# A ninth weight buffer in the room of the attention's buffers, the last w_down chunks in halves, and a split combine

## The chip, the cores and the metric

The kernel runs on one core of a Trainium2 chip. The metric is the time of one launch on the device in microseconds (us). The core has a matrix engine (TensorE, PE in the rows; its weight loads are PEld), a vector engine (VectorE, DVE), an activation engine (ScalarE, ACT), GpSimd (POOL) and SyncE (SP), which here issues every transfer (DMA) from the device's memory (HBM). The engines run their own lists of instructions and wait for each other by semaphores. SBUF is the memory on the core, with 128 partitions; matmul results go to PSUM, eight banks of 128 x 512 floats.

## What is computed

A trunk of two layers on 256 tokens of width 1024. Each layer is an attention (layer 0: a mix of three branches; layer 1: plain causal attention over one block, as there is only one) and then a mixture of experts, each followed by a layer norm of a residual sum. The change concerns the experts:

```
def grouped_moe(h, router_w, router_bias, w_gate, w_up, w_down):
    ...
    for e in range(N_EXPERTS):          # 16 experts, 2 chosen for each token
        he = jax.nn.silu(xt @ w_gate[e]) * (xt @ w_up[e])
        out = out + (he @ w_down[e]) * gate[:, e:e + 1]

def reference(x, ...):
    for layer in range(DEPTH):          # 2
        mix = nsa_mixer(...) if layer == 0 else moba_mixer(...)
        x = layer_norm(DN_ALPHA * x + mix, ...)
        ffn = grouped_moe(x, router_w, router_bias, w_gate[layer], w_up[layer], w_down[layer])
        x = layer_norm(DN_ALPHA * x + ffn, ...)
```

All is float32. `w_gate` and `w_up` are 1024 x 512 for each expert, `w_down` is 512 x 1024: 2 MiB each, 96 MiB for a layer's experts, all of which are read.

## The kernel before

**The ring.** Weights pass through `ring`, eight slots of 2 MiB (a chunk: 16 KB in each of 128 partitions). `STREAM` lists all chunks in the order of their loading: nine of layer 0's attention, 48 of its experts (`("moe", 0)` to `("moe", 47)`), eight of layer 1's attention (`("unit", 7)` to `("unit", 14)`), 48 of its experts. Chunk number c of the stream goes to slot c % 8, and SyncE issues its load when the chunk eight places before it has been used (`slot_free`, `wait_consumed`). An expert chunk is one DMA (L336), an attention chunk two of 1 MB (L313). Each slot has two semaphores for landings, one for each half; an expert chunk uses the first alone.

**The experts' rounds.** A stage has eight rounds (`PAIRS`), each of two experts, whose tokens (up to 64 each) are computed side by side in two halves of the array. A round takes six chunks, k = 0 to 5: w_gate of both experts, w_up of both, w_down of both. So chunk 6 i + k belongs to round i. On the TensorE a round (`experts`) is

- 32 matmuls with w_gate (`to_hidden`, L612), transposes of the gates of its slots (L618);
- 32 matmuls with w_up (L612);
- `combine` of the round before (L640): 8 matmuls that add its results to the tokens in PSUM banks 4 to 7, four for each half w of the columns;
- transposes of the hidden rows (L623), after the DVE has multiplied them (L1238); the DVE then copies them (L1241);
- in rounds 0 to 5 gathers of tokens for later rounds (L602);
- 32 matmuls with w_down (`from_hidden`, L630), for which ACT (L841) and the DVE (L1249) then make a scaled high part and the rest, one instruction for each half w;
- in rounds 0 to 5 more gathers.

The w_down block goes through the row blocks k and in each through both column halves w; in the last round it does all of w = 0 first, so that ACT and DVE can begin with that half in the middle of the block. After round 7 comes a last `combine`, then the layer norm.

**Before the stage.** Attention uses two further buffers, `R5` and `R6` (3072 floats in each partition): probabilities, transposed probabilities, staging for the rotary part, and last `OT`, its result, in the upper part of both. The output matmuls (`mix_out`, L562) read `OT` and count up `L.mix`, to 4 in a layer. The layer norms keep their weights in the first 2048 floats of `R5`; the experts keep `GP`, gate values by slot, in the first 512 of `R6`. SyncE issues expert chunks 0 to 5 early, and 6 and 7 behind the attention's last probabilities; both wait for `mix_out`, since their slots hold its weights. Then it waits for the layer norm (`x_ready`), loads the weights of the next one, and goes on with chunk 8, which waits for round 0's gate matmuls (`gate_done`).

## Time and profile before

| | us |
|---|---|
| median of 3 runs | 820.42 |
| lowest, highest | 819.17, 820.86 |
| the profiled execution | 817.06 |
| its span | 815.3 |
| TensorE busy in it | 754.2 |

The profile is of one execution. Its span is the time between the first and the last instruction of the core; 1.8 us lie outside it. All moments below are counted from the span's start. Layer 0's expert stage runs on the TensorE from 205.9 to 423.5 us, layer 1's from 586 to 804.7. A block of 32 matmuls stands in the rows as one row with its start, its duration and, in brackets, how long the engine was idle before it and what ended that.

### The profile page before, as it was taken

How to read it: one execution, taken by the hardware profiler on the slowest of the kernel's cores; microseconds unless marked ns; L12 is line 12 of the kernel's file. 1: busy time of each engine (PE TensorE's matmuls, PEld its weight loads, DVE VectorE, ACT ScalarE, POOL GpSimd, SP SyncE). 2: the span in 40 equal slices, each digit the busy share in tenths (PEclk: the TensorE clock that was granted, in tenths of full speed). 3: DMA queues.
4: the chain of work that ended last, by engine and by line, in shares of the span. 5: the costliest groups of instructions: out<-in, count | busy, mean ns of one | idle time of the engine just before them, and what ended most of it. 6: DMA issues, size and time to landing. Idle time of an engine off the chain costs nothing.

```text
span 815.3 us, 9027 instructions
## 1 busy us (share of the span) xinstructions
PE 754.2 (93%) x3713; PEld 402.3 (49%) x3713; DVE 282.5 (35%) x564; ACT 187.8 (23%) x435; POOL 88.0 (11%) x96
## 2 busy tenths in 40 slices
PE   5999999998999999998878999899899999998884
PEld 4877855545434444343236887555634344443331
DVE  3594365326212211111146874523521122111114
ACT  3443456312111001100004445612200110011000
POOL 0011234312000000000000320411200000000000
PEclk9999789999999999999997999999899999999997
DMA  9999400106599999999999854013489999999981
GB/s 297 366 391 411 188 1 2 52 15 243 201 430 427 428 429 426 428 427 427 429 388 386 328 207 174 34 52 110 148 353 427 428 428 425 430 427 428 428 347 53
DMA packets 38924, 245.03 MB, mean 301 GB/s; under 512 B 5344, under 2 KB 9568, under 8 KB 26592
## 3 DMA queue, kind: packets, MB, share of 16 engines
q1 hardware_dynamic: 38880, 244.41, 74.2%
q8 instruction: 32, 0.52, 0.3%
q14 instruction: 12, 0.10, 0.0%
HBM read 243.35 MB, written 1.05 MB: 300 GB/s over the span
## 4 chain that ended last, share of the span: by engine, by line
PE 79%; DMA 8%; DVE 7%; ACT 3%; issue 2%; POOL 0%; DVEq 0%; SPq 0%
PE ps L612 24%; PE ps L630 12%; DMA ring<-in_w_up 8%; PE ps L562 7%; PE ps L435 5%; PE ps L436 4%; PE ps L437 4%; PE ps L602 3%; PE ps L640 3%; PE ps L484 2%; ACT R L943 2%; PE ps L472 2%; PE ps L593 1%; PE ps L569 1%; PE ps L418 1%
## 5 line engine op out<-in xcount | busy, mean ns | idle before, releaser
L612 PE MATMUL ps<-ring,R 128*64 128x512 f32 x1024 | 229.9, 602 | 17.4 <-DMA ring<-in_w_up 7.9
L612 PEld LDWEIGHTS ps<-ring,R 128*64 128x64 f32 x1024 | 75.4, 138 | 150.6 <-issue 149.0
L630 PE MATMUL ps<-ring,R 128*64 128x512 f32 x512 | 113.4, 595 | 3.1 <-DVE R L1241 3.1
L841 ACT ACTIVATE wh<-ps,small 128x512 fp32r<-128x512 f32 x32 | 22.0, 687 | 276.1 <-PE ps L630 274.5
L1078 DVE TENSOR_TENSOR wl<-ring,wh 128x512 fp32r<-128x512 f32 x88 | 66.5, 770 | 48.3 <-ACT wh L819 48.1
L435 PE MATMUL ps<-wh,xh 128*128 128x512 f32 x176 | 71.9, 409 | 5.0 <-DVE wl L1078 4.9
L436 PE MATMUL ps<-wl,xh 128*128 128x512 f32 x176 | 70.4, 400 | 0.0
L437 PE MATMUL ps<-wh,xl 128*128 128x512 f32 x176 | 70.4, 400 | 0.0
L630 PEld LDWEIGHTS ps<-ring,R 128*64 128x64 f32 x512 | 35.3, 137 | 69.6 <-issue 64.0
L819 ACT CAST wh<-ring 128x512 fp32r<-128x512 f32 x88 | 54.3, 621 | 58.3 <-PE ps L437 58.3
L1249 DVE SCALAR_TENSOR_TENSOR wl<-ps,small,wh 128x512 fp32r<-128x512 f32 x32 | 24.0, 751 | 104.3 <-ACT wh L841 103.6
L562 PE MATMUL ps<-ring,R 128*128 128x512 f32 x128 | 56.8, 597 | 0.0
L1238 DVE TENSOR_TENSOR R<-R,ps 128x512 f32<-128x512 f32 x16 | 17.2, 1075 | 114.3 <-PE ps L612 114.3
L1245 DVE TENSOR_SCALAR wl<-ps 128x256 fp32r<-128x256 f32 x16 | 6.8, 424 | 115.4 <-PE ps L618 115.4
L943 ACT ACTIVATE R<-ps,small 128x128 f32<-128x128 f32 (+1 forms) x96 | 39.0, 419 | 29.7 <-DVE small L1128 29.7
L435 PEld LDWEIGHTS ps<-wh,xh 128*128 128x128 f32 x176 | 33.8, 192 | 15.0 <-DVE xl L1073 4.9
L986 POOL TENSOR_TENSOR R<-wh,small 128x512 f32<-128x512 f32 x8 | 8.3, 1043 | 284.6 <-PE ps L618 272.0
L437 PEld LDWEIGHTS ps<-wh,xl 128*128 128x128 f32 x176 | 33.6, 191 | 8.2
L436 PEld LDWEIGHTS ps<-wl,xh 128*128 128x128 f32 x176 | 33.8, 192 | 7.7
L562 PEld LDWEIGHTS ps<-ring,R 128*128 128x128 f32 x128 | 23.7, 190 | 27.6 <-issue 26.8
L1128 DVE TENSOR_REDUCE small<-ps 128x2 f32<-128x256 f32 (+1 forms) x48 | 24.5, 553 | 35.7 <-PE ps L472 35.7
L1011 POOL TENSOR_TENSOR R<-R 128x512 f32<-128x512 f32 (+1 forms) x16 | 23.3, 1459 | 123.9 <-DVE R L1121 123.9
(152 smaller groups left out, 812.9 us busy)
## 6 DMA issues: line engine op xcount, KB each, us to landing
ring<-in_w_gate SPq DMA_DIRECT2D x32, 2048.0 KB, 18.7
ring<-in_w_up SPq DMA_DIRECT2D x32, 2048.0 KB, 20.1
ring<-in_w_down SPq DMA_DIRECT2D x32, 2048.0 KB, 22.5
ring<-in_w_in SPq DMA_DIRECT2D x22, 1024.0 KB, 14.0
ring<-in_w_out SPq DMA_DIRECT2D x8, 1024.0 KB, 14.9
ring<-in_cmp_kw SPq DMA_DIRECT2D x2, 1024.0 KB, 16.3
ring<-in_cmp_vw SPq DMA_DIRECT2D x2, 1024.0 KB, 13.3
R<-in_ln_g SPq DMA_DIRECT2D x4, 512.0 KB, 5.1
```

Of the source, the lines that this page charges most:

```text
L435: mm(to, xh[:, j, tok], wh[:, c % WBUF], start=(j == 0), stop=False)
L436: mm(to, xh[:, j, tok], wl[:, c % WBUF], start=False, stop=False)
L437: last = mm(to, xl[:, j, tok], wh[:, c % WBUF], start=False, stop=(j == KJ - 1))
L562: last = mm(ps[:, 2 * a + w, :], OT[j][:, a * P:(a + 1) * P], in_slot(("unit", u))[:, j * UNIT:(j + 1) * UNIT], start=False, stop=(j == KJ ...
L602: last = mm(ps[:, bank, at * n:(at + 1) * n], Xp[k][:, a, j, :], Pm[:, a].rearrange("p e c -> p (e c)")[:, 0:n], start=(a == 0 and k == 0) ...
L612: last = mm(ps[64 * e:64 * e + 64, to, :], xe[:, j, at + 64 * e:at + 64 * e + 64], slots[e][:, j * UNIT:(j + 1) * UNIT], start=(j == 0), s ...
L630: last = mm(ps[64 * e:64 * e + 64, 2 + w, :], hT[:, k, 64 * e:64 * e + 64], slots[e][:, at:at + UNIT], start=(k == 0), stop=(k == FJ - 1))
L640: last = mm(ps[:, 4 + 2 * a + w, :], PmT[:, b, a, :], Yp[k][w], start=False, stop=(k == 1), skip_group_check=True)
L819: copy(wh[:, c % WBUF], in_slot(("unit", u))[:, j * UNIT:(j + 1) * UNIT]).then_inc(w_hi, 1)
L943: last = nc.scalar.activation(to, ps[:, 2 * (m % 2) + a, c:c + w], ACT.Exp, bias=nmax[:, m % 2, t, a:a + 1], accum_out=sums[:, m % 3, t, a ...
L1078: tt(wl[:, c % WBUF], in_slot(("unit", u))[:, j * UNIT:(j + 1) * UNIT], wh[:, c % WBUF], ALU.subtract).then_inc(w_lo, 1)
L1128: last = nc.vector.tensor_reduce(nmax[:, m % 2, t, :], ps[:, b:b + 2, t * P:t * P + (t + 1) * P], AX.X, ALU.max, negate=True)
```

## The change

- `R5` and `R6` become the two parts of one buffer `R56` of 6144 floats. Its last 4096 floats (the last third of `R5` and all of `R6`) are a ninth slot, `extra`. `GP` moves to the last quarter of `R4`.
- `places_of_stream` gives each chunk its slot. Chunk 8 of each expert stage goes to the ninth slot, which nothing of the stream held before; it waits until `L.mix` has reached 4. From then on each chunk takes the slot of the chunk nine before it. When attention chunks come, the ninth slot leaves the rotation.
- SyncE issues chunk 8 right behind chunk 7, ahead of its wait for the layer norm.
- The last two chunks of a stage, w_down of both experts of round 7, are loaded in halves of 1 MB (rows of the block k = 0, 1 first, for both experts, then k = 2, 3). The w_down block of round 7 goes through the halves one after the other, in each through w = 0 and w = 1, and waits for the second halves in its middle.
- In rounds 6 and 7 `combine` is split: its half w = 0 stays where it was, its half w = 1 comes behind the transposes of the hidden rows.

```diff
+        R56 = sb("R56", [P, 6 * D])
+        R5, R6 = R56[:, 0:3 * D], R56[:, 3 * D:6 * D]
+        extra = R56[:, 2 * D:6 * D]
...
-        GP = R6[:, 0:512].rearrange("p (a e c) -> p a e c", a=T, e=4)
+        GP = R4[:, 3 * FE:4 * FE].rearrange("p (a e c) -> p a e c", a=T, e=4)
...
+        LASTDOWN = 6 * PAIRS - 2
+
+        def places_of_stream():
+            slots, before, line = [], [], [(None, n) for n in range(SLOT)]
+            for what in STREAM:
+                if what[0] == "moe" and what[1] % (6 * PAIRS) == SLOT:
+                    held, n = None, SLOT
+                else:
+                    if what[0] != "moe":
+                        line = [x for x in line if x[1] != SLOT]
+                    held, n = line.pop(0)
+                slots.append(n)
+                before.append(held)
+                line.append((what, n))
+            return slots, before
+
+        SLOT_OF, BEFORE = places_of_stream()
+        in_halves = lambda what: what[0] != "moe" or what[1] % (6 * PAIRS) >= LASTDOWN
...
             def slot_free(what):
-                if AT[what] >= SLOT:
-                    wait_consumed(sp, STREAM[AT[what] - SLOT])
+                if BEFORE[AT[what]]:
+                    wait_consumed(sp, BEFORE[AT[what]])
+                elif SLOT_OF[AT[what]] == SLOT:
+                    l = what[1] // (6 * PAIRS)
+                    sp.wait_ge(L.mix, base[l].mix + 2 * T)
...
+                if in_halves(what):
+                    if k == 5:
+                        for h in range(2):
+                            for e in range(2):
+                                to = ("moe", n - 1 + e)
+                                c = slice(2 * D * h, 2 * D * (h + 1))
+                                sp.dma_start(in_slot(to)[:, c], expert_src(l, 2 * i + e, 2)[:, c]).then_inc(landing(to, h)[0], 16)
+                    return
                 sp.dma_start(in_slot(what), expert_src(l, 2 * i + k % 2, k // 2)).then_inc(landing(what, 0)[0], 16)
...
-                for n in range(ahead, 8):
+                for n in range(ahead, SLOT + 1):
                     load_expert(6 * PAIRS * l + n)
                 sp.wait_ge(N.x_ready, ready(2 * l, T - 1, 1))
                 load_ln(2 * l + 1, R.ln_in)
-                for n in range(8, 6 * PAIRS):
+                for n in range(SLOT + 1, 6 * PAIRS):
                     load_expert(6 * PAIRS * l + n)
...
                     if i:
-                        combine(rd, (i - 1) % 2, (2 * n - 1, 2 * n))
+                        combine(rd, (i - 1) % 2, (2 * n - 1, 2 * n), range(2) if more else (0,))
                     pe.wait_ge(rd.h, n + 1)
                     transpose_hidden(rd)
                     if more:
                         pe.wait_ge(rd.onehot, g + 2)
                         gather(rd, 1, (2 * part, 2 * part + 1), 4 * SLOTS)
+                    else:
+                        combine(rd, (i - 1) % 2, (2 * n - 1, 2 * n), (1,))
...
-                    from_hidden(rd, slots[4:6], [(k, w) for k in range(FJ) for w in range(2)] if i < PAIRS - 1 else
-                                [(k, w) for w in range(2) for k in range(FJ)])
+                    if i < PAIRS - 1:
+                        from_hidden(rd, slots[4:6], [(k, w) for k in range(FJ) for w in range(2)])
+                    else:
+                        from_hidden(rd, slots[4:6], [(k, w) for h in range(2) for w in range(2) for k in (2 * h, 2 * h + 1)],
+                                    chunks[4:6])
```

SyncE's list before, from the attention's end of layer 0 into the first rounds. The words in brackets name the semaphores waited for: `pt` counts the attention's transposed probabilities, `mix` its output matmuls, `ln_x_ready` the layer norm, the last three the gate, up and w_down blocks:

```order
L340 DMA R<-in_ln_g 128x1024 [waits pt]
L341 DMA R<-in_ln_b 128x1024
L336 DMA ring<-in_w_gate 128x4096 [waits mix] x2
L340 DMA R<-in_ln_g 128x1024 [waits ln_x_ready]
L341 DMA R<-in_ln_b 128x1024
L336 DMA ring<-in_w_up 128x4096 [waits gate_done_main] x2
L336 DMA ring<-in_w_down 128x4096 [waits up_done_main] x2
L336 DMA ring<-in_w_gate 128x4096 [waits y_main] x2
```

And after (the ninth slot shows as `R`):

```order
L372 DMA R<-in_ln_g 128x1024 [waits pt]
L373 DMA R<-in_ln_b 128x1024
L368 DMA ring<-in_w_gate 128x4096 [waits mix] x2
L368 DMA R<-in_w_up 128x4096 [waits mix]
L372 DMA R<-in_ln_g 128x1024 [waits ln_x_ready]
L373 DMA R<-in_ln_b 128x1024
L368 DMA ring<-in_w_up 128x4096 [waits gate_done_main]
L368 DMA ring<-in_w_down 128x4096 [waits gate_done_main]
L368 DMA ring<-in_w_down 128x4096 [waits up_done_main]
L368 DMA ring<-in_w_gate 128x4096 [waits up_done_main]
```

One w_up chunk stands ahead of the layer norm's wait now, and the pairs that wait for one block are shifted by one chunk.

The TensorE in round 7 of layer 0 before, from the end of the w_up block (L612) to the last combine (L640):

```order
L612 MATMUL ps<-ring,R 64x512 x15
L640 MATMUL ps<-wh,wl 128x512 [waits y_lo_main]
L640 MATMUL ps<-wl 128x512
L640 MATMUL ps<-wh,wl 128x512
L640 MATMUL ps<-wl 128x512
L640 MATMUL ps<-wh,wl 128x512 [waits y_lo_main]
L640 MATMUL ps<-wl 128x512
L640 MATMUL ps<-wh,wl 128x512
L640 MATMUL ps<-wl 128x512
L623 MATMUL ps<-cst,R 128x128 [waits h_main]
L623 MATMUL ps<-cst,R 128x128 x3
L630 MATMUL ps<-ring,R 64x512 [waits landed7_0,landed0_0,gsum_main,ht_sb_main]
```

And after, from the same block's end (L675 is `combine`, L655 the transposes, L665 the w_down block):

```order
L675 MATMUL ps<-wh,wl 128x512 [waits y_lo_main]
L675 MATMUL ps<-wl 128x512
L675 MATMUL ps<-wh,wl 128x512
L675 MATMUL ps<-wl 128x512
L655 MATMUL ps<-cst,R 128x128 [waits h_main]
L655 MATMUL ps<-cst,R 128x128 x3
L675 MATMUL ps<-wh,wl 128x512 [waits y_lo_main]
L675 MATMUL ps<-wl 128x512
L675 MATMUL ps<-wh,wl 128x512
L675 MATMUL ps<-wl 128x512
L665 MATMUL ps<-ring,R 64x512 [waits landed2_0,landed3_0,gsum_main,ht_sb_main]
L665 MATMUL ps<-ring,R 64x512 x7
```

Four of the eight combine matmuls moved behind the transposes. The lists of ACT and the DVE are the same as before but for the names of slots.

## Rows read from the trace of the kernel before

**Rows 1.** The page: header, TensorE's busy time, and GB/s in 40 slices.
```profile
span 815.3 us, 9027 instructions
...
PE 754.2 (93%) x3713; PEld 402.3 (49%) x3713; DVE 282.5 (35%) x564; ACT 187.8 (23%) x435; POOL 88.0 (11%) x96
...
GB/s 297 366 391 411 188 1 2 52 15 243 201 430 427 428 429 426 428 427 427 429 388 386 328 207 174 34 52 110 148 353 427 428 428 425 430 427 428 428 347 53
```

**Rows 2.** Chain of waits, 335 to 436 us: start, duration, what.
```profile
371.41 31.98 DMA ring<-in_w_up
```

**Rows 3.** Timeline of PE, layer 0's last rounds: start, duration, matmuls [idle before].
```profile
344.34 7.09 PE L612 MATMUL ps<-ring,R 128*64 128x512 f32 x32 [1.64 <-issue]
...
373.75 7.09 PE L612 MATMUL ps<-ring,R 128*64 128x512 f32 x32 [2.38 <-DMA ring<-in_w_up]
...
393.73 8.68 PE L612 MATMUL ps<-ring,R 128*64 128x512 f32 x32 [2.53 <-DMA ring<-in_w_gate]
...
403.53 7.09 PE L612 MATMUL ps<-ring,R 128*64 128x512 f32 x32 [0.75 <-DMA ring<-in_w_up]
...
413.90 7.09 PE L630 MATMUL ps<-ring,R 128*64 128x512 f32 x32 [0.78 <-DVE R L1241]
```

**Rows 4.** Timeline of PE, round 7 of layer 1.
```profile
773.19 7.09 PE L612 MATMUL ps<-ring,R 128*64 128x512 f32 x32 [2.11 <-DMA ring<-in_w_gate]
...
782.99 8.61 PE L612 MATMUL ps<-ring,R 128*64 128x512 f32 x32 [2.34 <-DMA ring<-in_w_up]
...
794.86 7.09 PE L630 MATMUL ps<-ring,R 128*64 128x512 f32 x32 [0.79 <-DVE R L1241]
```

**Rows 5.** Timeline of SyncE's queue: issues of chunks 6, 7 and 8, 9.
```profile
181.32 9.86 SPq L336 DMA_DIRECT2D ring<-in_w_gate  x2
...
213.06 0.80 SPq L336 DMA_DIRECT2D ring<-in_w_up  x2
```

**Rows 6.** Busy time by stretch; last three columns: clock, DMA share, GB/s.
```profile
210.00:214.00 4.00, 4.00 (x22) 1.26 (x18) 0.58 (x2) 0.60 (x1) 0.00 (x0) 1.00 0.00 0
232.00:342.00 110.00, 110.00 (x534) 44.77 (x530) 20.04 (x30) 10.25 (x17) 2.09 (x2) 1.00 1.01 428
```

**Rows 7.** Issues of ring in four stretches, each with its time to landing.
```profile
L336 SPq DMA_DIRECT2D ring<-in_w_gate x1: 328/328/328, 190.8 to 190.8; - x1
...
DMA to landing us min/median/max: 8.0/8.0/8.0
...
L336 SPq DMA_DIRECT2D ring<-in_w_up x2: 327/376/425, 371.0 to 371.4; - x2
...
DMA to landing us min/median/max: 27.5/29.7/32.0
...
L336 SPq DMA_DIRECT2D ring<-in_w_down x2: 328/380/432, 380.9 to 381.2; - x2
...
DMA to landing us min/median/max: 27.4/29.7/32.0
...
L313 SPq DMA_DIRECT2D ring<-in_w_in x2: 382/552/721, 391.2 to 391.7; - x2
...
DMA to landing us min/median/max: 24.7/25.8/27.0
```

**Rows 8.** Busy time by stretch at layer 1's last w_up block; columns as rows 6.
```profile
783.00:787.00 4.00, 4.00 (x12) 1.38 (x14) 0.00 (x0) 0.00 (x0) 0.00 (x0) 0.61 0.99 422
```

**Rows 9.** Timeline of all engines in round 7 of layer 0.
```profile
410.73 1.10 DVE L1238 TENSOR_TENSOR R<-R,ps 128x512 f32<-128x512 f32 x1 [7.16 <-PE ps L612]
...
412.52 0.60 PE L623 MATMUL ps<-cst,R 128*128 128x128 f32 x4
...
413.16 0.69 DVE L1241 COPY R<-ps 128x512 f32<-128x512 f32 x1 [1.33 <-PE ps L623]
...
421.04 0.69 ACT L841 ACTIVATE wh<-ps,small 128x512 fp32r<-128x512 f32 x1 [2.69 <-PE ps L630]
...
421.76 0.75 DVE L1249 SCALAR_TENSOR_TENSOR wl<-ps,small,wh 128x512 fp32r<-128x512 f32 x1 [2.62 <-ACT wh L841]
```

More of the change, by code:

```diff
@@ L111, in build @@
         R4 = sb("R4", [P, T * D])
-        R5 = sb("R5", [P, 3 * D])
-        R6 = sb("R6", [P, 3 * D])
+        R56 = sb("R56", [P, 6 * D])
+        R5, R6 = R56[:, 0:3 * D], R56[:, 3 * D:6 * D]
+        extra = R56[:, 2 * D:6 * D]
         small = sb("small", [P, 832])
@@ L194, in build @@
         x_in, ident_in, c_in, s_in = sem("x_in"), sem("ident_in"), sem("c_in"), sem("s_in")
-        landed = [[sem(f"landed{s}_{h}") for h in range(2)] for s in range(SLOT)]
+        landed = [[sem(f"landed{s}_{h}") for h in range(2)] for s in range(SLOT + 1)]
         w_hi, w_lo, w_used = sem("w_hi"), sem("w_lo"), sem("w_used")
@@ L238, in build @@
         AT = {what: c for c, what in enumerate(STREAM)}
+        LASTDOWN = 6 * PAIRS - 2
[14 more added lines that the diff above has]
+        in_halves = lambda what: what[0] != "moe" or what[1] % (6 * PAIRS) >= LASTDOWN
         def in_slot(what):
-            return ring[:, AT[what] % SLOT]
+            n = SLOT_OF[AT[what]]
+            return ring[:, n] if n < SLOT else extra
         def landing(what, h):
             c = AT[what]
-            n = sum(1 for b in range(c % SLOT, c + 1, SLOT) if h == 0 or STREAM[b][0] != "moe")
-            return landed[c % SLOT][h], 16 * n
+            n = sum(1 for b in range(c + 1) if SLOT_OF[b] == SLOT_OF[c] and (h == 0 or in_halves(STREAM[b])))
+            return landed[SLOT_OF[c]][h], 16 * n
         def wait_consumed(eng, what):
@@ L624, in transpose_hidden, with from_hidden @@
                 last.then_inc(rd.ht, 1)
-            def from_hidden(rd, slots, order):
-                for k, w in order:
+            def from_hidden(rd, slots, order, second=None):
+                for n, (k, w) in enumerate(order):
+                    if second and n == 4:
+                        for to in second:
+                            pe.wait_ge(*landing(to, 1))
                     for e in range(2):
@@ L633, in from_hidden, with combine @@
                         last.then_inc((rd.y0, rd.y)[w], 1)
-            def combine(rd, b, counts):
-                for w in range(2):
+            def combine(rd, b, counts, ws=range(2)):
+                for w in ws:
                     pe.wait_ge(rd.y_lo, counts[w])
```

## The prediction

> **What bounds the kernel now.** I read the page first: its header and the line of GB/s in 40 slices [rows 1]. The TensorE is busy 93% of 815.3 us, so one would look for matmuls to save; but the GB/s line says that in two long stretches (slices 12 to 20 and 31 to 38, in the two expert stages) the transfers run flat at about 428 GB/s. Two resources are near full there, and which of them ends the stage has to be read from its end. For that I took the chain of waits over the end of layer 0's experts [rows 2]: one link, 31.98 us from the issue of the last w_up chunk to 403.4 us, is a transfer. The timeline of the TensorE shows the same from its side [rows 3]: from round 5 of 8 on it stands idle before blocks of 32 expert matmuls, 1.64, 2.38, 2.53 and 0.75 us, and the releaser of the last three is a chunk of weights (for the first the row shows none; nothing else is missing there but a chunk). Layer 1 repeats it 380 us later [rows 4]. So each expert stage begins bound by the TensorE (which starts with eight chunks in the ring) and ends bound by the transfers. The other engines are no candidates: they wait for the TensorE throughout.
>
> What sets the end of the transfers? The SyncE's list [rows 5]: chunks 6 and 7 of the stage are issued at 181.32 and 9.5 us later (the row's 9.86 us span both, the second's issue being the last 0.33), then nothing until 213.06, when round 0's gate block has freed the first slots. In that gap the transfers stand still: 0 GB/s in 210 to 214 us [rows 6]. From 213 us on they never pause (428 GB/s over 232 to 342 us). Landing times, worked out as issue plus time to landing [rows 7]: the last two w_up chunks at 371.03 + 27.5 = 398.5 and 371.41 + 32.0 = 403.4, the last two w_down chunks at 380.87 + 27.4 = 408.3 and 381.24 + 32.0 = 413.2 us. The step is **4.9 us per chunk**, and it holds for the whole stage: a lone chunk takes 8.0 us from issue to landing [rows 7], 3.1 more than a step, so chunk 8 landed at 213.06 + 8.0 = 221.1, and the 39 steps to 413.2 average 4.93. So the last landing is 213 us plus the latency plus as many steps as chunks are still to come.
>
> **The change part by part.** *Ninth buffer.* Chunk 8 of each stage no longer waits for the gate block of round 0 but for the attention's last output matmul, as chunk 7 does, and is issued right behind it. It lands one step behind chunk 7 (190.8 + 8.0 = 198.8), at 204 us, in a gap that lasts to 213 [rows 5, 6]: its transfer is hidden. On the SyncE it stands ahead of two small loads (layer-norm weights, which the DVE needs at the end of the stage, 200 us later) and adds no wait that chunk 7 hasn't. From 213 us on 39 chunks are left, not 40; the slot for each comes from the chunk nine before, and the stream is never short of a free slot: the order of freeing is the same, one chunk later in number. So each landing from there on comes **4.9 us** earlier. Is the TensorE early enough to use it? Its waits on chunks up to the last w_up block add up to 1.64 + 2.38 + 2.53 + 0.75 = 7.3 us [rows 3]; 4.9 of these may go before it becomes the bound, and 2.4 are left. In layer 1 the waits before the last gate and up blocks are 2.11 and 2.34 [rows 4], 4.5 us by themselves, and earlier ones come on top. So the last up block starts at 403.53 - 4.9 = 398.6 in layer 0. Value 4.9 per layer; 0 is the floor if nothing lands earlier, and more than 4.9 is excluded as one chunk is moved.
>
> *Split of combine in rounds 6 and 7.* After the up block (over at 403.53 + 7.09 = 410.6) the TensorE runs 8 combine matmuls, done at 412.5, then the transposes of the hidden rows from 412.52; but the DVE had the hidden rows ready at 410.73 + 1.10 = 411.83 [rows 9]. With 4 of the 8 ahead (1.0 us) the TensorE is free at 411.6, waits for the DVE and transposes from 411.87: 0.65 us sooner. The DVE copies the transposes 0.64 us behind their start and takes 0.69 [rows 9], to 413.20; the TensorE runs the other 4 combine matmuls meanwhile, from about 412.35 to 413.35. So the last w_down block starts at 413.35 where it was 413.90: **0.55 us** gained. From below 0 bounds it, if the second half of the combine costs all of it; from above 0.65. I take 0.55, as every piece has its row. In round 6 the split gains nothing: the next gate block waits for its chunk (2.53 us [rows 3]).
>
> *Halves of the last two w_down chunks.* Without them the w_down block could start when both have landed, 413.2 - 4.9 = 408.3; the TensorE gets there at 398.6 + (413.35 - 403.53) = 408.4. The two nearly coincide, so the halves save nothing if all goes as worked out, and make sure that the split's 0.55 is kept: the first halves land by 403.4, the second by 408.3, and the second are needed only after half the block, 3.5 us later. Their cost: four issues where two were, some 0.4 us each on a queue with nothing urgent behind it, and perhaps slower packets. The nearest rows are the 1 MB loads of w_in, the first two of which land at 391.2 + 24.7 = 415.9 and 391.7 + 27.0 = 418.7 [rows 7], 2.7 to 2.8 us apart where half a chunk's step is 2.45. Four at 2.8 take 11.2 for 9.8: 1.4 us, inside the 3.5 of cover. Value 0; what would make it a loss is rival D.
>
> The Trainium skill has a rule against this part: by "SBUF — State Buffer", section "The DMA setup-cost knee", each transfer pays a fixed 2 us or so beside its bytes, and one large transfer is to be preferred. By it two more transfers would bring the last landing to 412.3, 0.4 us behind the 411.9 at which it is needed. The sum would then be 0.8 us less gain in both layers together. The rows speak against it: chunks that stand in the queue land 4.9 us apart where a lone one takes 8.0 [rows 7], so the fixed part is paid once.
>
> *Order of the last block.* Column half 0 is now finished after three quarters of the block, not after one half, 1.75 us before its end. ACT and DVE need 0.69 and 0.75 us for it [rows 9] and some 0.1 of signals, so it is ready 0.2 us before the block's end. No cost; were it missed, 0.2.
>
> *Moved buffer GP and the next layer's loads.* GP goes to another free place with the same instruction; 0. The loads of layer 1's first weights (issued from 391.2 on [rows 7]) now wait for a chunk one earlier and come behind the last w_down: they land 4.9 us sooner, as all does. 0.
>
> **Sum.** 2 x (4.9 + 0.55) = 10.9 us. The profiled execution took 817.06 (span 815.3), so it would take 806.2. The runs shown have their median at 820.42, 3.4 us over the profiled one; nothing in the sum depends on where these 3.4 lie, so I subtract from the median: **809.5 us**.
>
> **What may disturb it: the clock.** The granted clock falls to its lower level (1.2 for 2.4 GHz) behind some of the waits: in layer 0 the gate block behind the 2.53 us wait took 8.68 us and not 7.09 [rows 3]; in layer 1 it was the last up block, 8.61 us behind 2.34 us [rows 4], with the clock at 0.61 over 783 to 787 us [rows 8]. Waits of 2.38 and 2.11 us had no such effect. The first fall was absorbed by the next wait for a chunk; the second was paid in full, 1.52 us, since behind the last up block nothing waits for a transfer any more. After the change the wait before that block is 9.8 - 7.09 - 0.44 = 2.3 us as before, in both layers. So anything from no fall paid (808.0) to both (811.0) can come; one, as now, is the middle.
>
> **Rivals.**
> A, only the buffer pays: the second part of the combine or a late w_down eats the 0.55. 820.42 - 9.8 = 810.6. For it: the two times that nearly coincide (408.3 and 408.4). Against: halves.
> B, one fall of the clock more is paid on the last blocks or in the routing between attention and experts, and the split gives nothing: 810.6 + 1.5 = 812.1.
> C, each half costs 1.0 us beside its bytes, a third of the 3.1 that a lone chunk shows over its step: the last one lands at 408.3 + 4.0 = 412.3, 0.4 us late in each layer, 809.5 + 0.8 = 810.3. For it: the w_in loads' 0.3 each, which is too little; against it: the queued chunks. This is also where the skill's rule above would end.
> D, slower: the halves do not overlap, and each of the four pays the 3.1 us that a lone chunk shows over its step [rows 7]. They then take 4 x (2.45 + 3.1) = 22.2 us behind the last w_up chunk, and the last lands at 398.5 + 22.2 = 420.7, where it is needed at 411.9: 8.8 us late per layer, against a gain of 5.45. That gives 820.42 + 2 x 3.35 = 827.1. It decides from 411.9 + 5.45 = 417.4 on, that is if each half costs some 2.3 us beside its bytes. Against it speak all queued chunks, 4.9 us apart.
> E, the change does not do what it says: the ninth chunk is not away before 213 us, because SyncE stands elsewhere. Only the split is left: 820.42 - 1.1 = 819.3. Against: the SyncE was free at about 191.5 us.
>
> **How the numbers follow.** Chances: forecast 0.65 (808.0 to 811.0 with the clock's share), A 0.15, B 0.12, C 0.03, D 0.02, E 0.03. The range takes in the forecast with a fall less and its rounding (1.5 more below for what the median's distance from the profile leaves open) and A, B and C above: 806.5 to 813.0. It leaves out D, E and a little of each tail. Faster by over 0.2% (1.6 us, about what a measurement of this kernel can tell from no change) are the forecast, A, B and C: 0.95; same is E: 0.03; slower is D: 0.02.
>
> **What would show it.** In the profile after: a ninth chunk issued beside chunk 7 and no pause shorter than before 213; last w_up chunk landing near 398.5 in layer 0, last up block starting there; 4 combine matmuls, transposes, 4 combine matmuls, and 9.8 us from the last up block's start to the w_down block's where it was 10.4; layer 1 shifted by 5.4 at its start and the last w_down block by 10.9. I am wrong if the TensorE no longer waits for chunks in rounds 6 and 7 (then it is the bound, and less than 4.9 was to be had), if the stream after 213 us has pauses, or if the waits are the same and blocks longer.

## The result

The changed kernel takes 809.05 us (median of 4 runs, 805.87 to 809.25), the kernel before, on the same chip, 820.64 (819.17 to 820.92). The ratio is 0.9861, 95% interval 0.9841 to 0.9881: 11.4 us less by the ratio and 11.6 between the medians, where 10.9 were forecast, and the time is 0.5 us from the 809.5 predicted.

The page of after shows the same kernel with the same flat stretches in the transfers:

```profile
span 807.4 us, 9035 instructions
...
PE 757.7 (94%) x3713; PEld 404.5 (50%) x3713; DVE 282.3 (35%) x564; ACT 187.8 (23%) x435; POOL 88.0 (11%) x96
...
GB/s 301 365 394 379 231 2 1 1 52 242 190 431 428 428 427 426 428 426 427 425 397 387 400 160 157 105 53 98 267 251 429 427 427 427 429 427 427 427 388 54
```

SyncE's queue, timeline of after, which answers to [rows 5]:

```profile
184.13 9.86 SPq L368 DMA_DIRECT2D ring<-in_w_gate  x2
194.03 0.43 SPq L368 DMA_DIRECT2D R<-in_w_up  x1
197.46 0.33 SPq L372 DMA_DIRECT2D R<-in_ln_g  x1
197.83 0.45 SPq L373 DMA_DIRECT2D R<-in_ln_b  x1
217.22 0.33 SPq L368 DMA_DIRECT2D ring<-in_w_up  x1
217.59 7.34 SPq L368 DMA_DIRECT2D ring<-in_w_down  x2
```

The third issue, `R<-in_w_up`, is chunk 8, at 194.03, and the view of this one issue has its time to landing:

```profile
L368 SPq DMA_DIRECT2D R<-in_w_up x1: 432/432/432, 194.0 to 194.0; - x1
...
DMA to landing us min/median/max: 12.6/12.6/12.6
```

At 206.6 it is there, 10.6 us before the next issue. The two small loads are issued 3.4 us behind it, still in the pause. That is the forecast picture.

The end of layer 0's stage, timeline of PE in after, answers to [rows 3] and [rows 9] (L644 is `to_hidden`, L655 the transposes, L675 `combine`, L665 `from_hidden`):

```profile
393.36 8.64 PE L644 MATMUL ps<-ring,R 128*64 128x512 f32 x32 [2.70 <-DMA ring<-in_w_gate]
...
403.16 0.62 PE L644 MATMUL ps<-R 128*64 128x512 f32 x1 [0.80 <-DMA ring<-in_w_up]
...
411.50 0.66 PE L655 MATMUL ps<-cst,R 128*128 128x128 f32 x4
411.91 0.48 PE L675 MATMUL ps<-wh,wl 128*128 128x512 f32 x1
...
413.01 7.09 PE L665 MATMUL ps<-ring,R 128*64 128x512 f32 x32
```

Here the TensorE still waits for chunks in round 7, so the stage is bound by the transfers as before, one step earlier. From the last w_up block (403.16) to the last w_down block (413.01) it is 9.85 us where it was 10.37. The last w_up chunk lands 192.9 us behind the start of layer 0's stage where it was 197.5, and 191.9 behind that of layer 1's where it was 196.8: 4.5 and 4.9 us earlier. Layer 1's last gate block fell to the lower clock in this run, and not its last up block:

```profile
767.34 8.78 PE L644 MATMUL ps<-ring,R 128*64 128x512 f32 x32 [2.62 <-DMA ring<-in_w_gate]
```

**Where the profiled span moved.** Both profiles can be cut at the first gate block of each stage and the last w_down block (the stretch between them is called the stretch below). A stage starts with the row of its first gate block, here in after's timeline, where it was 205.93 before:

```profile
210.09 7.09 PE L644 MATMUL ps<-ring,R 128*64 128x512 f32 x32
```

| piece of the span | before | after | difference |
|---|---|---|---|
| start to layer 0's stage | 205.93 | 210.09 | +4.16 |
| stretch, layer 0 | 207.97 | 202.92 | -5.05 |
| to layer 1's stage | 172.11 | 172.08 | -0.03 |
| stretch, layer 1 | 208.85 | 201.87 | -6.98 |
| rest | 20.4 | 20.4 | 0.0 |

The sum is -7.9 and not -10.9, because the part ahead of the first stage, of whose instructions none was changed, took 4.2 us more. Its cause stands in the clock column (last but two) of the busy time by stretch. Before:

```profile
80.00:115.00 35.00, 33.94 (x248) 0.76 0.31 131
195.00:206.00 11.00, 9.40 (x64) 0.84 0.52 194
```

and after:

```profile
80.00:115.00 35.00, 34.00 (x232) 0.71 0.34 145
195.00:210.00 15.00, 12.14 (x68) 0.77 0.84 334
```

The TensorE was granted less clock there in this execution. Matched matmul by matmul, after falls behind before in three places only: by 1.4 us between 15 and 17 us (matmuls 0.45 us apart in before are 0.85 apart in after), by 1.5 between 84 and 87, and by 1.5 between 195 and 203. How much of these stretches runs at the lower clock differs from one execution to the next. It was so in all the profiles below too: layer 0's stage began between 203.97 and 210.25 us in kernels whose instructions up to there are the same but for SyncE's issue of chunk 8. That issue isn't the cause either: without the early chunk the stage began at 203.97 to 210.25 us (four profiles), with it at 204.90 to 210.17 (ten). The median over several runs averages this, one profile doesn't: the two stretches are the better measure of the change. In layer 1, 1.52 of the 6.98 are the fall that [rows 4] showed on before's last up block, gone from there in this run, so the change itself made 5.05 and 5.46 us.

### The profile page after: what moved, and what is told of

Same layout as the page of the kernel before. It is cut to its first block, busy times and chain, and to the rows that moved or that the text cites. A ratio compares the mean times of both kernels' runs of the same rounds, so it can differ in the third digit from the quotient of the medians.

```text
span 807.4 us, 9035 instructions
## 1 busy us (share of the span) xinstructions
PE 757.7 (94%) x3713; PEld 404.5 (50%) x3713; DVE 282.3 (35%) x564; ACT 187.8 (23%) x435; POOL 88.0 (11%) x96
## 4 chain that ended last, share of the span: by engine, by line
PE 80%; DMA 8%; DVE 7%; ACT 3%; issue 2%; DVEq 0%; SPq 0%
PE ps L644 24%; PE ps L665 12%; DMA ring<-in_w_up 7%; PE ps L594 7%; PE ps L467 5%; PE ps L468 5%; PE ps L469 4%; PE ps L634 3%; PE ps L675 3%; ACT R L983 2%; PE ps L504 2%; PE ps L516 2%; PE ps L625 1%; PE ps L607 1%; PE ps L450 1%
## 5 line engine op out<-in xcount | busy, mean ns | idle before, releaser
L644 PE MATMUL ps<-ring,R 128*64 128x512 f32 x928 | 230.0, 603 | 5.3 <-DMA ring<-in_w_gate 5.3
L644 PEld LDWEIGHTS ps<-ring,R 128*64 128x64 f32 x928 | 72.2, 139 | 115.9 <-issue 114.0
L665 PE MATMUL ps<-ring,R 128*64 128x512 f32 x448 | 113.4, 596 | 0.8 <-DMA ring<-in_w_down 0.8
L665 PEld LDWEIGHTS ps<-ring,R 128*64 128x64 f32 x448 | 35.4, 137 | 67.4 <-issue 63.5
L644 PE MATMUL ps<-R 128*64 128x512 f32 x96 | 42.4, 595 | 1.4 <-DMA ring<-in_w_up 1.4
```

Of the source, the lines that this page charges most:

```text
L644: last = mm(ps[64 * e:64 * e + 64, to, :], xe[:, j, at + 64 * e:at + 64 * e + 64], slots[e][:, j * UNIT:(j + 1) * UNIT], start=(j == 0), s ...
L665: last = mm(ps[64 * e:64 * e + 64, 2 + w, :], hT[:, k, 64 * e:64 * e + 64], slots[e][:, at:at + UNIT], start=(k == 0), stop=(k == FJ - 1))
```

## The experiments

The runs were made in five groups, each on one chip together with the kernel before; "before" is its median in that group, and times of different groups are compared by their ratios. The time is the measure for the whole. The stretch is the measure for parts of a microsecond; it comes from one profiled execution of each kernel, and where the same kernel was profiled twice (after), the two differ by 0.26 and 0.08 us.

| kernel | time us | before | ratio (95%) | stretch 0 | stretch 1 |
|---|---|---|---|---|---|
| before | - | - | - | 207.97 | 208.85 (fall) |
| after | 809.05 | 820.64 | 0.9861 (0.9841 to 0.9881) | 202.92 | 201.87 |
| after once more | 807.57 | 820.49 | 0.9836 (0.9810 to 0.9862) | 202.66 | 201.95 |
| ninth buffer only | 808.32 | 820.01 | 0.9857 (0.9827 to 0.9887) | 203.29 | 202.79 |
| split only | 817.53 | 820.01 | 0.9968 (0.9947 to 0.9989) | 207.67 | 206.88 |
| without halves | 808.94 | 820.01 | 0.9866 (0.9835 to 0.9897) | 202.75 | 202.02 |
| ninth late | 824.18 | 820.01 | 1.0066 (1.0040 to 1.0091) | 212.78 (fall) | 210.35 |
| ninth late, clean | 818.52 | 820.49 | 0.9974 (0.9956 to 0.9993) | 207.62 | 206.98 |
| chunks 9, 10 in halves | 806.85 | 820.49 | 0.9837 (0.9811 to 0.9864) | 202.28 | 201.41 |
| chunks 9, 10 in quarters | 805.43 | 820.49 | 0.9812 (0.9786 to 0.9837) | 201.85 | 201.64 |
| chunks 9 to 14 in halves | 804.98 | 821.16 | 0.9800 (0.9766 to 0.9833) | 201.97 (fall) | 200.75 (fall) |
| chunks 9 to 20 in halves | 806.72 | 821.16 | 0.9824 (0.9793 to 0.9855) | 201.23 (fall) | 201.50 (fall) |
| w_up of round 7 in halves | 808.25 | 821.21 | 0.9851 (0.9831 to 0.9870) | 201.89 | 199.57 |
| 9 to 14 and w_up in halves | 796.57 | 821.21 | 0.9720 (0.9696 to 0.9744) | 197.96 | 196.62 |

"Fall" marks a stretch whose last up block ran in part at the lower clock.

### One part alone

**The ninth buffer alone.** The changed kernel with two things put back:

```diff
-        in_halves = lambda what: what[0] != "moe" or what[1] % (6 * PAIRS) >= LASTDOWN
+        in_halves = lambda what: what[0] != "moe"
...
-                        combine(rd, (i - 1) % 2, (2 * n - 1, 2 * n), range(2) if more else (0,))
+                        combine(rd, (i - 1) % 2, (2 * n - 1, 2 * n))
...
-                    else:
-                        combine(rd, (i - 1) % 2, (2 * n - 1, 2 * n), (1,))
...
-                        from_hidden(rd, slots[4:6], [(k, w) for h in range(2) for w in range(2) for k in (2 * h, 2 * h + 1)],
-                                    chunks[4:6])
+                        from_hidden(rd, slots[4:6], [(k, w) for w in range(2) for k in range(FJ)])
```

> The ninth buffer with its early chunk alone; w_down chunks whole, combine unsplit. The measure that the clock disturbs least is the stretch from the start of round 0's gate block to the start of round 7's w_down block, 207.97 us in layer 0 of before and 208.78 in layer 1 (1.52 of them a fall of the clock on the last up block). Theory (the early chunk shifts the whole stream by one step, the split adds 0.55 per layer): stretch about 203.1 to 203.4 in layer 0, time 9.8 us under before, about 810.8. Rival (the split carries a good part of the gain): less than 8 us under before.

Measured: 203.29 in layer 0, 4.68 us under before, 202.79 in layer 1, 4.54 under before without its fall, and 808.32 us, ratio 0.9857. The buffer with its early chunk carries nearly the whole change.

**The split alone**, in the kernel before: `combine` takes the halves as an argument, and rounds 6 and 7 call it with (0,) ahead of the transposes and (1,) behind them.

> The kernel before with combine split in rounds 6 and 7 and nothing else. Theory: the last w_down block starts 9.8 us behind the start of the last up block where it is 10.37, if its chunk is there. Without the ninth buffer the last w_down chunk lands 9.8 us behind the last w_up chunk, so the gain is 0.4 to 0.55 us per layer, 0.8 to 1.1 in the time: about 819.7, hardly more than the spread of the runs. Rival: 0, because the chunk is late; then the row of the w_down block names a transfer as its releaser.

Measured: stretches of 207.67 and 206.88, that is 0.30 and 0.45 us gained (with 1.52 for the fall taken off layer 1's 208.85). The last up block and the w_down block of layer 0, in PE's timeline:

```profile
406.83 7.09 PE L612 MATMUL ps<-ring,R 128*64 128x512 f32 x32 [2.35 <-DMA ring<-in_w_up]
...
416.69 7.09 PE L630 MATMUL ps<-ring,R 128*64 128x512 f32 x32
```

9.86 us, no idle piece named. The last w_down chunk was issued at 384.3 with 32.3 us to landing:

```profile
L336 SPq DMA_DIRECT2D ring<-in_w_down x2: 328/380/431, 383.9 to 384.3; - x2
...
DMA to landing us min/median/max: 27.7/30.0/32.3
```

So it lands at 416.6, 0.1 us before the block: the near coincidence that the prediction worked out is there. The time, 817.53, is 2.5 us under before, 2.6 by the ratio, with an interval of 0.9 to 4.3 us, and the 0.75 us of the two stretches lie just under it. The runs scatter between 814.85 and 821.16 us. I take the stretch to be the size of the split; where the rest of the time comes from is not shown.

**Without the halves**, the changed kernel with the first and the last piece of the diff above.

> The changed kernel with the last two w_down chunks whole again and the last block in its old order (all of column half 0 first). Theory: the last w_down block waits for its chunk for 0.1 us or less, since its landing (9.8 us behind the last w_up chunk) and the end of the transposes' copy coincide: time within 0.3 us of the changed kernel, 809.0. Rival (the halves carry what the split gives): 0.5 us per layer slower, 810.1, with a transfer as releaser of the block.

Measured: 808.94 us, stretches 202.75 and 202.02, which is after's to 0.2 us. From the last up block (401.67) to the w_down block it is 9.87 us, with no idle piece:

```profile
411.54 7.09 PE L665 MATMUL ps<-ring,R 128*64 128x512 f32 x32
```

The last chunk, whole, was issued at 378.7 with 32.7 us to landing, 411.4. The halves bring nothing where they stand, as forecast.

### Early or deep?

The ninth buffer does two things: chunk 8 starts early, and from then on nine chunks can be held and not eight. To tell these apart, chunk 8 was held back to round 0's gate block, with the nine slots kept:

```diff
                 elif SLOT_OF[AT[what]] == SLOT:
                     l = what[1] // (6 * PAIRS)
                     sp.wait_ge(L.mix, base[l].mix + 2 * T)
+                    wait_consumed(sp, ("moe", 6 * PAIRS * l))
```

> The changed kernel, nine slots and all, but chunk 8 waits for round 0's gate block as it did before: the ring is as deep as in the changed kernel and only the early start is taken away. Theory (what counts is how many bytes are still to come when the stream starts): the 4.9 us per layer are gone, stretch 207.4 in layer 0, time about 819.5. Rival (a deeper ring helps by itself, as the stream never lacks a slot): the gain stays, about 809 to 811.

Neither was right: 824.18 us, 4.2 us slower than before. SyncE's timeline shows what I had overlooked:

```profile
211.15 0.33 SPq L369 DMA_DIRECT2D R<-in_w_up  x1
211.52 0.43 SPq L373 DMA_DIRECT2D R<-in_ln_g  x1
212.00 0.43 SPq L374 DMA_DIRECT2D R<-in_ln_b  x1
212.47 0.88 SPq L369 DMA_DIRECT2D ring<-in_w_up  x1
```

The wait for the layer norm and its two loads stand behind chunk 8 on SyncE. In the changed kernel they follow it into the pause; here they were held back with it and lay inside the stream. In layer 0 the chunk behind them took 15.0 us to landing and landed 8.1 us behind chunk 8, where a step is 4.9:

```profile
L369 SPq DMA_DIRECT2D ring<-in_w_up x1: 879/879/879, 212.5 to 212.5; - x1
DMA to landing us min/median/max: 15.0/15.0/15.0
```

1 MB written by two loads, each of one row of 4 KB spread over 128 partitions, cost the stream 3.2 us there, and 4.0 in layer 1. The prediction had these loads down as harmless, which holds in the pause only.

**Ninth late, clean**: chunk 8 also issued behind the two loads.

```diff
-                for n in range(ahead, SLOT + 1):
+                for n in range(ahead, SLOT):
...
-                for n in range(SLOT + 1, 6 * PAIRS):
+                for n in range(SLOT, 6 * PAIRS):
```

> The ring of nine slots with chunk 8 issued where it was before, behind the loads of the layer norm's weights and behind round 0's gate block. The first form of this experiment had the two loads behind chunk 8 in the queue, inside the stream, and so confounded two things. Theory: the two loads cost it 3.2 us per layer, which go; the early start is away, so the stretch is that of the kernel before with the split, 207.4 to 207.7 in layer 0, and the time 818 to 819.5. Rival (a deeper ring helps by itself): 809 to 813.

Measured: stretches 207.62 and 206.98, those of the split alone (207.67 and 206.88) to 0.1 us, and 818.52 us. Against the first form the two loads cost the stage 3.6 us in layer 0 (212.78 without its fall of 1.5, less 207.62) and 3.4 in layer 1. A ninth slot without the early chunk is worth nothing (its time, like the split's, is about 2 us under before and not 0.75); the early start is worth 207.62 - 202.66 = 4.96 and 206.98 - 201.95 = 5.03 us. The changed kernel of the same group of runs:

> The changed kernel once more, on the same chip as the three others, to compare them with. Theory: 0.986 of the kernel before; stretches 202.9 and 201.9 us but for 1.5 us where the clock falls on a last block.

It gave 807.57 us, 0.9836 (0.9810 to 0.9862), and stretches within 0.3 us of the first profile's. By its ratio the change is worth 13.5 us (11.3 to 15.6), 2 us more than in the first group with the same stretches.

### Can the stream start still earlier?

If the end of the stage is the start of the stream plus steps, the same trick goes on: chunks 9 and 10 wait for the whole gate block, though its first rows free parts of their slots sooner. They were loaded in pieces (PIECES = 2, then 4), each issued when the TensorE has passed that part of the block:

```diff
+                        for q in range(PIECES):
+                            if q < PIECES - 1:
+                                sp.wait_ge(gate_part, l * (PIECES - 1) + q + 1)
+                            else:
+                                slot_free(what)
+                            for m in (n - 1, n):
+                                i, k = divmod(m % (6 * PAIRS), 6)
+                                c = slice(8 // PIECES * UNIT * q, 8 // PIECES * UNIT * (q + 1))
+                                sp.dma_start(in_slot(("moe", m))[:, c], expert_src(l, 2 * i + k % 2, k // 2)[:, c]).then_inc(landing(("moe", m), 0)[0], 16)
```

> The changed kernel, and chunks 9 and 10 (which take the slots of round 0's two gate chunks) are loaded in two pieces of 1 MB each: the first pieces as soon as the gate block has passed the first half of its rows, 3.5 us before its end. Theory (the stream is the bound from its start on, and each us by which it starts earlier comes off the end until the TensorE is the bound): stretch of the stage 202.9 - 3.5 = 199.4 in layer 0, time 7 us under the changed kernel, about 802. Rival (the TensorE is the bound by now): less than 2 us per layer.

> The same with four pieces of 512 KB for each of the two chunks, the first after a quarter of the gate block, 5.3 us before its end. The TensorE's own time for the stretch, with no wait for a chunk, is 25.4 + 5 x 25.98 to the gate block of round 6, 24.3 for that round, 7.4 + 9.85 for the last two steps: 196.9 us. Theory: 202.9 - 5.3 = 197.6, just above that bound; time about 10.6 us under the changed kernel, 798.5. Rival (small pieces cost more than they bring): not under the kernel with halves.

Both expectations were far off: halves gained 0.4 us in layer 0 and 0.5 in layer 1, quarters 0.8 and 0.3. The stream did start 3.4 us (halves) and 5.2 us (quarters) earlier, but then stood short of a free slot. Busy time by stretch of the kernel with quarters (clock, DMA share, GB/s at the end):

```profile
215.00:220.00 5.00, 5.00 (x26) 1.64 (x24) 0.76 (x2) 0.60 (x1) 0.00 (x0) 1.00 1.00 374
220.00:225.00 5.00, 4.81 (x22) 1.57 (x19) 1.07 (x1) 0.00 (x0) 0.00 (x0) 1.00 0.97 342
225.00:230.00 5.00, 5.00 (x29) 2.33 (x29) 1.38 (x2) 0.00 (x0) 0.00 (x0) 1.00 0.89 374
230.00:240.00 10.00, 10.00 (x52) 3.88 (x50) 1.50 (x2) 1.96 (x3) 0.00 (x0) 1.00 0.97 380
```

where the second profile of after has 433, 426 and 431 GB/s over 220 to 240 us. Chunk 11 cannot be issued before the up block of round 0 is over, 14.5 us behind the stage's start, and chunk 13 not before its w_down block, 24.4 us. In layer 0 of the kernel with quarters the last quarter had landed at 16.2 us and chunk 11 at 22.4, chunk 12 at 27.3, and chunk 13 came 8.0 us later, at 35.3, exactly when it also landed in the changed kernel; in layer 1 it came at 34.4, 0.8 us before. So each release is a floor of its own for the end, and the floor of chunk 13 lies within a us of that of chunk 9. Not all of that floor is understood: chunk 13 took 10.9 us from issue to landing, where chunk 11 took 7.9; 2.9 us of transfers were left ahead of the one and 1.7 ahead of the other. With 8 us it would have landed at 32.4, and why it didn't was not found out. The size of the pieces isn't it: quarters that stand in the queue land 1.2 to 1.3 us apart, 5.1 for 2 MB where a whole chunk takes 4.9, and halves 2.5.

**Round 0's slots all in halves** (chunks 9 to 14, each first piece issued half a block earlier), and the same for rounds 0 and 1 (chunks 9 to 20):

> The changed kernel, and the six chunks 9 to 14, which take the slots that round 0 frees, come in two pieces of 1 MB, the first as soon as the gate, up or w_down block has passed its first half. The run with chunks 9 and 10 alone in pieces gained 0.4 to 0.5 us per layer and not 3.5, since the stream ran short at chunk 11, which waits for the end of the up block. Theory (each free slot in turn is a floor for the end of the stream: its moment plus the steps still to come; the next floors are chunks 11 and 13): with those in pieces too the floor is chunk 15, issued 32.5 us behind the stage's start, so the stretch falls from 202.7 to about 200.2 in layer 0, and the time is 5 us under the changed kernel on the same chip. Rival (pieces lower the stream's rate, 380 for 428 GB/s where they stood): less than 1 us per layer.

> The same for the slots of rounds 0 and 1, chunks 9 to 20. Theory: the only floor left is chunk 9 itself, 3.5 us earlier than in the changed kernel: stretch about 199.3 in layer 0, 1 us under the run with round 0 alone, with the TensorE's own 196.9 still below it. Rival (pieces lower the rate): longer than with round 0 alone.

With chunks 9 to 14 the stream behaved as expected: the last w_up chunk landed 190.3 us (layer 0) and 189.1 us (layer 1) behind the stage's start, where the second profile of the changed kernel has 192.7 and 192.0. Yet only 0.7 of these 2.4 us and 1.2 of these 2.9 reached the stretch. The last up block, in PE's groups of 398 to 407 us and in the busy time by stretch:

```profile
L660 PE MATMUL ps<-ring,R 128*64 128x512 f32 x16 | 8.8, 713 | 0.0
L660 PE MATMUL ps<-R 128*64 128x512 f32 x16 | 8.7, 710 | 2.3 <-DMA ring<-in_w_up 2.3
```

```profile
398.40:407.00 8.60, 8.59 (x32) 0.80 1.00 411
388.60:396.00 7.40, 7.38 (x34) 1.00 0.99 420
```

Its matmuls took 0.71 us and not 0.59, at a mean clock of 0.80: the clock fell behind the wait of 2.33 us ahead of the block, and the w_down block came 11.54 us behind the up block, not 9.84. That is 1.7 us, paid in full, in both layers of both kernels; without it the stretches of the first are 200.3 and 199.0 us, where 200.2 was expected. In the changed kernel the last gate block waits longest (2.7 us) and takes the fall; what it loses, the next wait for a chunk absorbs (0.80 left of 2.3). Here the gate block waited 1.0 us only (in layer 1 not at all), kept its clock, and the fall came on the one block behind which nothing is left to absorb it. That it "moved" there is argued from these four stretches, not shown: in the kernel with quarters the gate blocks waited 2.61 and 2.39 us and the up blocks 2.33 and 2.33, and none of the four lost its clock. With rounds 0 and 1 in halves the stream was no earlier on the whole (last w_up landing 189.6 and 189.8 us behind the start), against the further 1 us expected, and the time, 806.72, not better than with round 0 alone.

### The block with no cover

That points at the wait itself: round 7's up block starts when its two chunks have landed whole, then runs 7.1 us with nothing to wait for. Load these two in halves, as the change does with w_down, and it can run its first half before the last landing:

```diff
-        in_halves = lambda what: what[0] != "moe" or what[1] % (6 * PAIRS) >= LASTDOWN
+        in_halves = lambda what: what[0] != "moe" or what[1] % (6 * PAIRS) >= LASTDOWN - 2
...
-                    if k == 5:
+                    if k in (3, 5):
...
+                    if j == KJ // 2:
+                        for what in second:
+                            pe.wait_ge(*landing(what, 1))
```

> The changed kernel with the last two w_up chunks in halves too: round 7's w_up block starts with the first halves and waits in its middle for the second. In the changed kernel that block waits 2.3 us for whole chunks, runs 7.1 us, and the last w_down block starts 9.84 us behind it, when its second halves have been there for 0.0 to 0.1 us and the first for 4.9. Theory (the halves of w_down bring nothing only because the w_up block ahead is bound by whole chunks): the w_up block ends 3.5 us behind the last w_up landing and not 7.1, so the w_down block starts 3.5 us earlier with its first halves and waits in its middle for the second, or not at all; its end moves from 16.9 to 13.4 us behind the last w_up landing. Both layers: 7 us under the changed kernel, about 801 to 802. Rival (the bound is now the w_down landing or the clock, which falls at one of the waits): 2 us per layer or less.

> Both: the slots of round 0 refilled in halves (its stream was 2.5 us earlier at the end, but in both layers the clock fell on the last w_up block, 1.7 us), and w_up of round 7 in halves. Theory: 2.5 + 3.5 us per layer, and the fall gone with the single wait: end of the last w_down block 203.5 us behind the stage's start where it is 209.8, time 794 to 798. Rival: the clock keeps the 1.7 us, 798 to 801.

Alone the halves of w_up gained 1.0 and 2.3 us in the stretch, where 3.5 were expected, and the time (0.9851) cannot be told from the changed kernel's. In layer 0 the reason is again the fall on the gate block, now with nothing behind it to absorb it; layer 1's gate block, the second row, kept its clock:

```profile
391.90 8.78 PE L647 MATMUL ps<-ring,R 128*64 128x512 f32 x32 [2.70 <-DMA ring<-in_w_gate]
...
767.00 7.09 PE L647 MATMUL ps<-ring,R 128*64 128x512 f32 x32 [2.66 <-DMA ring<-in_w_gate]
```

The first halves of w_up had landed at 396.8 (issued at 371.8 with 25.0 us to landing). At full clock the up block starts 7.38 us behind the gate block, as in layer 1 (767.00 to 774.38), so it could have started at 399.3; it started at 400.98, when the slowed gate block was over. In layer 1 the gain was 2.3 and not 3.5, since the gate block ahead still waits for whole chunks: it starts 182.35 us behind the stage's start, and 7.38 and 9.84 us of matmuls and copies behind it make the stretch of 199.57. The expectation had looked at the up block's wait alone.

Both edits together: **796.57 us** (795.25 to 801.06), 0.9720 (0.9696 to 0.9744) of the kernel before, and beyond the changed kernel's 0.9861 and 0.9836 by more than the intervals; 794 to 798 had been expected. The last rounds of layer 0 in PE's timeline, and the clock over them in both layers:

```profile
386.77 7.09 PE L663 MATMUL ps<-ring,R 128*64 128x512 f32 x32 [1.13 <-DMA ring<-in_w_gate]
393.79 0.44 PE L671 MATMUL ps<-cst,R 128*128 128x128 f32 x2
...
404.00 7.09 PE L686 MATMUL ps<-ring,R 128*64 128x512 f32 x32
```

```profile
386.00:415.00 29.00, 26.51 (x118) 10.35 (x118) 7.12 (x12) 2.35 (x4) 0.00 (x0) 1.00 1.02 407
757.00:785.00 28.00, 26.60 (x120) 10.07 (x118) 7.45 (x12) 2.89 (x5) 0.00 (x0) 1.00 0.66 276
```

One wait for a chunk, of 1.13 us in layer 0, is left, the clock stays at 1.00, and the stretches are 197.96 and 196.62 us, where the TensorE's own time without any wait was worked out as 196.9. So layer 1's expert stage is bound by the TensorE from end to end (it is idle for 0.4 us in all), and layer 0's is 1.13 us from it: there the last gate chunk still sets the end. Neither edit is worth much alone (0.9800 and 0.9851, with intervals that overlap the repeat's); together they take 10.0 us off the two stretches of the changed kernel. The rows fit this account: with round 0's slots alone the last up block waited 2.33 us for whole chunks and took the fall, with the halves of w_up alone the gate block ahead of it waited 2.7 us, and with both neither is left.

## Why the prediction was right

- **What bounds the stage.** Right: the transfers, from their restart on. The clean late ninth shows it: the same kernel with the chunk issued at the restart loses 4.96 and 5.03 us.
- **4.9 us per layer from the early chunk.** Right: 4.68 and 4.54 alone, and 4.96 and 5.03 against the clean late ninth. The last w_up chunk landed 4.5 and 4.9 us sooner.
- **0.55 us per layer from the split.** Right in mechanism and near in size: the distance between the last two blocks went from 10.37 to 9.85, 0.52 us; the stretch with the split alone moved by 0.30 and 0.45. The transposes started 8.34 us behind the last up block, to the hundredth as worked out.
- **0 from the halves.** Right: 0.2 us or less with and without. The four landed 2.5 us apart, half a step each, so the fixed part that the Trainium skill puts on each transfer ("SBUF — State Buffer", section "The DMA setup-cost knee") did not show for transfers that stand in a queue: rivals C and D are out. So is E, by the issue at 194.03, and A and B, in both of which the split gives nothing, by the 9.85. The 2.8 us apart that the prediction took from the w_in loads was too much. The new order of the last block cost nothing, as forecast: from its start to the end of the span it is 20.4 us before and after.
- **The clock.** Rightly named as what blurs the result, but placed too narrowly. I looked at the two last blocks alone; most of what differs between executions lies ahead of the first stage (4.2 us in the profiled pair). The forecast that layer 1 would start 5.4 us sooner failed by that: it started 0.9 sooner in the profile, and its last w_down block 7.9 sooner and not 10.9. And whether a fall is paid depends on where it lands: on the gate block, absorbed; on the up block, 1.5 to 1.7 us.
- **A slip that did no harm:** the two loads of layer-norm weights behind chunk 8 were counted as free because they are needed late. They are free because they fall into the pause; within the stream they cost the stage 3.4 to 3.6 us.
- **The closeness of the time** is in part luck. The sum of 10.9 is borne out by the stretches (5.05 + 5.46 = 10.5, plus one fall that before's profile pays and after's doesn't). But the ratio of the first group gives 11.4 us and that of the repeat 13.5, and no run shows where the 2 us between them lie.
- **A reading that left out a term:** the waits for chunks up to layer 0's last up block are not 7.3 us but 8.2, as the gate block of round 6 waits too. It did no harm, as the room was enough either way:

```profile
363.92 7.09 PE L612 MATMUL ps<-ring,R 128*64 128x512 f32 x32 [0.92 <-issue]
```

- **What the sum could not tell:** with the stream one step earlier, these waits looked like much room. But the first attempt to use more of it failed, as chunk 13 was a second floor just below the first. The prediction's picture, one start plus steps, held for the one step that the change takes and not for a second.

## To carry over

Where a stage ends on its transfers, its end is the largest, over all chunks, of the moment at which the chunk's slot comes free, plus that chunk's own time to landing (8 to 11 us here), plus the steps still to come. The ninth buffer paid because it let a chunk go in the pause ahead of the stage (5 us per layer), and not as one more buffer (0). When one such floor is taken away, work out the next before expecting the whole, and look at the wait just ahead of the last block: there whole chunks and a fall of the clock are paid in full. Halving the chunks of that block gave 1.0 and 2.3 us alone, and 4.0 and 4.1 us (a fall of 1.7 included) once the stream came earlier. For parts of a microsecond compare stretches within a stage, not the times of single executions.

## What the runs showed of the hardware

- In the expert stages the clock fell behind waits of 1.95 to 2.71 us of the TensorE, and not behind all of them. In before it fell behind 2.53 and 2.34 but not 2.38 and 2.11. The kernel with the ninth buffer only has a fall behind 2.13 us, the clean late ninth one behind 1.95. The last gate block kept its 7.09 us behind 2.70 us in layer 0 of two kernels (split only, clean late ninth) and behind 2.66 in layer 1 of the one with w_up in halves. So the length of the wait alone doesn't tell. A block on which the clock fell took 8.5 to 8.8 us for 7.09. Two of these rows, from the clean late ninth and from the ninth buffer only:

```profile
348.97 8.76 PE L645 MATMUL ps<-ring,R 128*64 128x512 f32 x32 [1.95 <-issue]
...
762.92 8.78 PE L644 MATMUL ps<-ring,R 128*64 128x512 f32 x32 [2.13 <-DMA ring<-in_w_gate]
```

- A 2 MB transfer issued into an idle queue lands after 7.8 to 8.5 us; in a full queue the step is 4.89 us, with single steps of 5.3 to 5.8. One issued with little left ahead of it can be worse than either: chunk 13 of the kernel with quarters was issued 2.9 us before chunk 12 landed and took 10.9 us. Why it is 10.9 and not 8 was not found out.
